# Expert weights in pieces of 256 rows by 1024 columns, two chunks at once, and a ScalarE loop that begins at the gathered copies

## What is computed

```
def moe_swiglu(h, router, w1, w3, w2):
    logits = (h @ router).astype(jnp.float32)
    top_vals, top_idx = lax.top_k(logits, TOP_K)
    top_w = jax.nn.softmax(top_vals, axis=-1)
    combine = jnp.sum(jax.nn.one_hot(top_idx, N_EXPERTS) * top_w[..., None], axis=-2)
    for e in range(N_EXPERTS):
        y = y + combine[..., e:e+1] * ((silu(h @ w1[e]) * (h @ w3[e])) @ w2[e])
```

## Time and profile before

| what | value |
|---|---|
| median of 3 runs | 1594.7 us (1590.41 to 1596.37) |
| profiled execution | 1590.57 us, span 1588.8 us |
| TensorE matmul (PE) busy | 1520.4 us, 96% |
| VectorE (DVE) busy | 1181.2 us, 74% |
| ScalarE (ACT) busy | 906.5 us, 57% |
| read from HBM | 424.31 MB |
| expert weights (ring<-in_moe_w) | 336 transfers of 1 MB |
| expert loop on TensorE | from 594 us to the last scatter at 1580 us |

### The profile page before, as it was taken

One profiled execution on the slowest core, in us unless ns is written; L12 is line 12 of the kernel. 1 busy time (PEld: TensorE's weight loads), 2 busy tenths in 40 slices (PEclk: granted clock), 3 DMA queues, 4 the chain that ended last, 5 costly groups with the idle time before them and its releaser, 6 DMA issues.

```text
span 1588.8 us, 19808 instructions
## 1 busy us (share of the span) xinstructions
PE 1520.4 (96%) x7386; PEld 1211.3 (76%) x7386; DVE 1181.2 (74%) x1148; ACT 906.5 (57%) x830; POOL 29.9 (2%) x44
## 2 busy tenths in 40 slices
PE   7987999998997889999999999999999999999998
PEld 5654599997654478888887888888888888888886
DVE  4974354453884348889888889888889888889895
ACT  1034243441013347777777777778777778777774
POOL 1010000000011000000000000000000000000000
PEclk9987999999996989999999999999999999999999
DMA  7540365635170039999999999998999999999992
GB/s 250 198 150 0 117 202 186 191 101 186 36 257 1 0 135 341 377 369 364 360 364 321 372 380 351 363 375 315 369 375 356 368 362 328 360 378 367 364 362 87
DMA packets 203556, 426.58 MB, mean 268 GB/s; under 512 B 7378, under 2 KB 48594, under 8 KB 203476
## 3 DMA queue, kind: packets, MB, share of 16 engines
q1 hardware_dynamic: 202160, 424.90, 74.5%
q10 hardware_dynamic: 1316, 0.49, 0.1%
HBM read 424.31 MB, written 1.05 MB: 268 GB/s over the span
## 4 chain that ended last, share of the span: by engine, by line
PE 89%; DVE 5%; issue 2%; ACT 2%; DMA 1%; POOL 0%; ACTq 0%; POOLq 0%; DVEq 0%; SPq 0%
PE bank L1520 13%; PE bank L1522 13%; PE bank L1521 13%; PE bank L1164 8%; PE bank L1544 6%; PE bank L1542 6%; PE bank L1543 6%; PE bank L1421 3%; PE bank L1422 3%; PE bank L1423 3%; PE bank L1351 2%; PE bank L1530 2%; PE bank L1439 1%; PE bank L1438 1%; PE bank L1437 1%
## 5 line engine op out<-in xcount | busy, mean ns | idle before, releaser
L761 DVE TENSOR_TENSOR w_split<-ring,w_split 128x2048 fp32r<-128x2048 f32 x369 | 843.1, 2290 | 201.6 <-ACT w_split L504 200.8
L504 ACT CAST w_split<-ring 128x2048 fp32r<-128x2048 f32 x369 | 705.4, 1914 | 287.7 <-PE bank L1522 160.0
L1520 PE MATMUL bank<-w_split,xe_hi 128*128 128x512 f32 x896 | 355.6, 397 | 6.9 <-DVE w_split L761 6.9
L1522 PE MATMUL bank<-w_split,xe_lo 128*128 128x512 f32 x896 | 350.3, 391 | 0.0
L1521 PE MATMUL bank<-w_split,xe_hi 128*128 128x512 f32 x896 | 349.7, 390 | 0.0
L1520 PEld LDWEIGHTS bank<-w_split,xe_hi 128*128 128x128 f32 x896 | 168.7, 188 | 42.7 <-DVE w_split L761 9.2
L1522 PEld LDWEIGHTS bank<-w_split,xe_lo 128*128 128x128 f32 x896 | 168.6, 188 | 36.4
L1521 PEld LDWEIGHTS bank<-w_split,xe_hi 128*128 128x128 f32 x896 | 168.8, 188 | 33.3
L1542 PE MATMUL bank<-w_split,actT_hi 128*128 128x512 f32 x448 | 175.2, 391 | 0.0
L1544 PE MATMUL bank<-w_split,actT_lo 128*128 128x512 f32 x448 | 174.5, 389 | 0.0
L1543 PE MATMUL bank<-w_split,actT_hi 128*128 128x512 f32 x448 | 174.4, 389 | 0.0
(11 more groups left out here) (229 smaller groups left out, 1362.1 us busy)
## 6 DMA issues: line engine op xcount, KB each, us to landing
ring<-in_moe_w SPq DMA_DIRECT2D x336, 1024.0 KB, 6.5
ring<-in_dense_w SPq DMA_DIRECT2D x33, 1024.0 KB, 5.3
ring<-in_w_in SPq DMA_DIRECT2D x8, 1024.0 KB, 10.1
ring<-in_w_in SPq DMA_DIRECT2D x4, 2048.0 KB, 13.9
ring<-in_w_out SPq DMA_DIRECT2D x4, 2048.0 KB, 13.7
ring<-in_cmp_k_w SPq DMA_DIRECT2D x2, 2048.0 KB, 16.1
ring<-in_cmp_v_w SPq DMA_DIRECT2D x2, 2048.0 KB, 8.3
ring<-in_w_in SPq DMA_DIRECT2D x2, 1120.0 KB, 14.9
```

The costliest lines, as they stand in the source:

```text
L504: nc.scalar.copy(split_part(0, t), raw(t)).then_inc(w_hi_ready, 1)
L761: V.tensor_tensor(split_part(1, t), raw(t), split_part(0, t).bitcast(F32), ALU.subtract).then_inc(w_lo_ready, 1)
L1520: T.matmul(dst, xe_hi[:, kk, own], hi[:, k, :], start=(kk == 0), stop=False)
L1522: last = T.matmul(dst, xe_lo[:, kk, own], hi[:, k, :], start=False, stop=(kk == KD - 1))
```

## The change

An expert's first and third matrix are read in pieces of 256 rows by 1024 columns, which serve two chunks at once (the seventh chunk stays alone, with pieces of 512 by 512). The chunks form four groups (0, 1), (2, 3), (4, 5), (6); e1 and e3 of a group fill two banks each. The order of pieces, the matmuls' order, the places of the gates, of the gate products, of the adds, of the scatter and of the selection follow from the groups. The scatter uses bank 4 in place of 3. On ScalarE the five gathered copies 3 to 7 move from the end of a loop turn to the head of the next, behind the small activation that names the silu table, and after the loop they stand once more.

Numbered from 0, the 42 pieces of an expert are then: e1(0, 1) 0 to 3, e3(0, 1) 4 to 7; e1(2, 3) 8 to 11, e2(0) 12, 13, e3(2, 3) 14 to 17, e2(1) 18, 19; e1(4, 5) 20 to 23, e2(2) 24, 25, e3(4, 5) 26 to 29, e2(3) 30, 31; e1(6) 32, 33, e2(4) 34, 35, e3(6) 36, 37, e2(5) 38, 39, e2(6) 40, 41.

```diff
-    expert_stream = [("e1", 0, 0), ("e1", 0, 1), ("e3", 0, 0), ("e3", 0, 1)]
-    for c in range(1, FCH):
-        expert_stream += [("e1", c, 0), ("e1", c, 1), ("e3", c, 0), ("e3", c, 1), ("e2", c - 1, 0), ("e2", c - 1, 1)]
-    expert_stream += [("e2", FCH - 1, 0), ("e2", FCH - 1, 1)]
+    groups = [tuple(range(c, min(c + 2, FCH))) for c in range(0, FCH, 2)]
+    expert_stream = []
+    for g, own in enumerate(groups):
+        before_it = groups[g - 1] if g else ()
+        for kind, n in (("e1", 0), ("e3", 1)):
+            expert_stream += [(kind, own[0], q) for q in range(2 * len(own))]
+            expert_stream += [("e2", c, half) for c in before_it[n:n + 1] for half in range(2)]
+    expert_stream += [("e2", FCH - 1, half) for half in range(2)]
...
-        BACK = (3, 5, 6, 7)
+        BACK = (4, 5, 6, 7)
...
-                        src = (w1 if kind == "e1" else w3)[:, 4 * half:4 * half + 4, c * BANK:(c + 1) * BANK]
-                        dst = raw(t).rearrange("p (k n) -> p k n", k=4)
+                        wide = len(groups[c // 2])
+                        k = 4 // wide
+                        src = (w1 if kind == "e1" else w3)[:, k * half:k * half + k, c * BANK:(c + wide) * BANK]
+                        dst = raw(t).rearrange("p (k n) -> p k n", k=k)
```

ScalarE:

```diff
-            for q in range(2 * QB):
+            for q in range(3):
                 gathered(0, q)
...
             with sc.Fori(0, pairs) as pair:
+                nc.scalar.activation(cstat[:, 1:2], ones[:, 0:1], ACT.Silu)
+                for q in range(3, 2 * QB):
+                    gathered(pair, q)
...
+                    for g, chunks in enumerate(groups):
+                        c, last = chunks[0], 2 * len(chunks) - 1
+                        if g >= 1:
+                            highs(done, past("e1", c, last // 2))
+                            actT_high(c - 2)
+                            done = past("e1", c, last // 2)
+                        highs(done, past("e1", c, last))
+                        done = past("e1", c, last)
+                        used("e1", c, last)
+                        for n in chunks:
+                            gate(n)
+                        if g >= 1:
+                            highs(done, past("e2", c - 2, 1))
+                            done = past("e2", c - 2, 1)
+                            actT_high(c - 1)
+                        if g == 2:
                             sc.wait_ge(selT_psum, nth(j, 1, 1))
...
-                    if h == PAIR - 1:
-                        for q in range(3, 2 * QB):
-                            gathered(pair + 1, q)
+            for q in range(3, 2 * QB):
+                gathered(pairs, q)
```

VectorE:

```diff
+                    def lows(first, end):
+                        for t in range(first, end):
+                            low_part(BASE + t, j)
+                            if t == 2:
+                                scaled_low(j)
+
+                    def past(kind, c, half):
+
+                        return min(xplace[kind, c, half] + SPLIT + 1, XS)
+
                     done = 0
-                    for c in range(FCH):
...
+                    for g, chunks in enumerate(groups):
+                        c, last = chunks[0], 2 * len(chunks) - 1
+                        if g >= 1:
+                            lows(done, past("e1", c, last // 2))
+                            actT_low(c - 2)
+                            done = past("e1", c, last // 2)
+                            lows(done, past("e2", c - 2, 1))
+                            done = past("e2", c - 2, 1)
                             actT_low(c - 1)
...
+                        ready = min(xplace["e3", c, last] + SPLIT, XS - 1)
+                        lows(done, ready)
+                        done = ready
+                        for n in chunks:
+                            dv.wait_ge(sg_ready, nth(j, FCH, n + 1))
+                            if n == c:
+                                used("e3", c, last)
+                            V.tensor_tensor(act[:, n % 2, :], sg[:, n % 2, :], bank[2 + n % 2][:],
+                                            ALU.mult).then_inc(act_ready, 1)
+                        if g == 0:
+                            add_back(j)
+                        if g == 1 and h == PAIR - 1:
+                            dv.wait_ge(selT_psum, nth(j, 1, 1))
+                            select(pair + 1)
```

TensorE (`select_rows` holds what stood at L1573 to L1579):

```diff
+                    up("e1", 0, range(4))
                     scatter(j)
-                    for c in range(1, FCH):
-                        up("e1", c)
+                    up("e3", 0, range(4))
+                    for c in range(2, FCH, 2):
+                        pieces = 2 * len(groups[c // 2])
+                        pe.wait_ge(sg_ready, nth(j, FCH, c))
+                        up("e1", c, range(pieces // 2))
+                        if c == 2:
+                            pe.wait_ge(added, nth(j, 4, 2))
+                        transposes(c - 2)
+                        up("e1", c, range(pieces // 2, pieces))
+                        if c == 2:
+                            pe.wait_ge(added, nth(j, 4, 5))
+                        down(c - 2, 0)
+                        down(c - 2, 1)
                         transposes(c - 1)
+                        up("e3", c, range(pieces))
...
                         down(c - 1, 1)
                         if c == 2:
+                            select_rows()
```

More of the change, by code:

```diff
@@ L669, in actT_high, with gate @@
                         nc.scalar.copy(actT_hi[:, c % 2, :], bank[4][:]).then_inc(actT_hi_ready, 1)
-                    done = 0
-                    for c in range(FCH):
[L673 to L683, removed]
+                    def gate(c):
                         if c >= 2:
@@ L686, in _, with highs @@
                         nc.scalar.activation(sg[:, c % 2, :], bank[c % 2][:], ACT.Silu).then_inc(sg_ready, 1)
-                        if c == 3:
+                    def highs(first, end):
+                        for t in range(first, end):
+                            high_part(BASE + t, j)
+                            if t == 2:
+                                scaled_high(j)
+                    def past(kind, c, half):
+                        return min(xplace[kind, c, half] + SPLIT + 1, XS)
+                    done = 0
+                    for g, chunks in enumerate(groups):
[14 more added lines that the diff above has]
+                        if g == 2:
                             sc.wait_ge(selT_psum, nth(j, 1, 1))
@@ L690, in _ @@
                             nc.scalar.copy(slot_weight[:], bank[7][:, S:S + 1]).then_inc(selT_ready, 1)
-                    while done < xplace["e2", FCH - 1, 0]:
-                        high_part(BASE + done, j)
-                        done += 1
+                    highs(done, xplace["e2", FCH - 1, 0])
                     if h == PAIR - 1:
@@ L1107, in actT_low @@
                                         ALU.subtract).then_inc(actT_ready, 1)
-                    done = 0
[L1110 to L1117, removed]
-                            actT_low(c - 1)
[L1119 to L1126, removed]
+                    def lows(first, end):
+                        for t in range(first, end):
+                            low_part(BASE + t, j)
+                            if t == 2:
+                                scaled_low(j)
@@ new lines, in past @@
+                    def past(kind, c, half):
+                        return min(xplace[kind, c, half] + SPLIT + 1, XS)
+                    done = 0
+                    for g, chunks in enumerate(groups):
[6 more added lines that the diff above has]
+                            done = past("e2", c - 2, 1)
+                            actT_low(c - 1)
+                        ready = min(xplace["e3", c, last] + SPLIT, XS - 1)
[8 more added lines that the diff above has]
+                        if g == 0:
@@ L1127, in _ @@
                             add_back(j)
-                        if c == 3 and h == PAIR - 1:
+                        if g == 1 and h == PAIR - 1:
                             dv.wait_ge(selT_psum, nth(j, 1, 1))
                             select(pair + 1)
-                    while done <= xplace["e2", FCH - 1, 0]:
-                        low_part(BASE + done, j)
-                        done += 1
+                    lows(done, xplace["e2", FCH - 1, 0] + 1)
                     actT_low(FCH - 1)
@@ L1510, in split_piece, with up @@
                         return split_views(t, k)
[L1512 to L1522, removed]
+                    def up(kind, c, pieces):
+                        wide = len(groups[c // 2])
+                        for q in pieces:
+                            hi, lo = split_piece(kind, c, q, 4 // wide)
+                            for k in range(4 // wide):
+                                kk = 4 // wide * q + k
+                                for n in range(wide):
```

(27 more changed lines are left out.)

## The result

The changed kernel took 1645.1 us (median of 4, 1644.1 to 1646.3) against 1595.4 for the kernel before on the same chip: a ratio of 1.0318, 95% interval 1.0295 to 1.0341 (a ratio here is estimated from all the runs; the quotient of the two medians is 1.0311). The forecast was 1644.

What follows compares the result with a forecast made beforehand. TensorE was taken to bound the kernel; waits of 14.1, 13.2 and 16.1 us plus 6.4 for the clock gave 49.8 on 1590.57, or 1640.4, and 4.1 more for the median: forecast 1644, own range 1630 to 1656, wider range 1614 to 1666.

Steps and rivals of the forecast that it cites:

- Wait A: Before piece 10, every expert: low 10 queues behind two gate products and four adds on VectorE; 1.77 us, eight times.
- Wait C: Before piece 34, every expert: VectorE subtracts the needed activations only after low 35; 2.01 us, eight times, 16.1 us.
- Wait B: Before piece 20, each pair's second expert: low 20 stands behind a selection awaiting TensorE; 3.31 us, four times, 13.2 us.
- The clock: TensorE's 3.2 us idle before piece 20 brings a half-clock stretch costing 1.6 us, four times, 6.4 us.
- Transfers, groups, bank 4 at 0: Longer transfer runs, places that hold despite the wider groups, and the scatter's new bank: each forecast to cost 0.
- ScalarE's head at 0: Between pairs: one table load per pair falls away but gains 0, because TensorE's own loop branch ends the gap.
- clock at all waits: Rival: half clock also follows the waits at pieces 10 and 34, up to 25.6 us more, 1670 us; chance 0.15.
- A and C covered: Rival: one more piece in hand hides the waits at pieces 10 and 34, giving 1614 us; chance 0.12.
- The transfers pace the loop: Rival: weight transfers limit the expert loop and hide TensorE's stalls, so time stays at 1594.7 us; chance 0.05.
- ScalarE at the heads: Rival: ScalarE's lateness at loop heads holds TensorE, VectorE's order costs nothing; 7.4 us gained, 1587.3 us; chance 0.03.

Runs made afterwards that it cites:

- e1: Not a run in the kept text: the matmuls with an expert's first matrix, as in e1(0, 1), pieces 0 to 3; no time of its own.
- e3: Not a run in the kept text: the matmuls with an expert's third matrix, as in e3(0, 1), pieces 4 to 7; no time of its own.
- fillers at all three: Changed kernel with unused identity transposes on TensorE before piece 10, before piece 34 and before piece 20 of the second expert; 1638.6 us, ratio 1.0299.
- all three edits: Changed kernel with selection one group later, scatter behind e3 and chunk 4's activations a piece earlier; 1594.8 us against 1592.3 for the kernel before, ratio 1.0014.
- the head alone: Kernel before with only ScalarE's new loop head (table-naming activation first, gathered copies 3 to 7 behind it); 1592.9 us against 1593.2, ratio 0.9994.
- again: The changed kernel unaltered, measured once more beside the kernel before on the same chip; 1648.1 us, ratio 1.0344.
- selection later: Changed kernel with VectorE writing the next pair's selection one group later, behind the subtraction of chunk 2's transposed activations; 1627.1 us, ratio 1.0227.
- last group: Changed kernel with chunk 4's transposed activations cast and subtracted one weight piece earlier, before the high and low part of piece 35; 1624.3 us, ratio 1.0202.
- filler at B: Changed kernel with 26 unused identity transposes in TensorE's wait at piece 20, second expert of each pair; 1640.5 us, ratio 1.0304.
- scatter back: Changed kernel with the scatter moved from between e1 and e3 of the first group to behind e3; 1636.2 us, ratio 1.0292.
- selection early: Kernel before with only VectorE's selection for the next pair moved from chunk 3 to chunk 2; 1615.8 us, ratio 1.0133.

## Why the prediction was right

- *TensorE bounds, so each wait counts in full.* Shown: taking away one wait at a time shortens the loop by 21.2, 21.4 and 12.6 us, and taking away all three brings back the 983.6 us. That the three numbers add up to just the 55.2 of the change is partly chance: each also holds what the clock did in that profile, and two of them the 1.6 us at the loop's start. The waits alone, 13.8, 16.5 and 14.2, are 44.5, against the 44.6 of the run with fillers at all three.
- *Wait A:* forecast 1.77 a time, 14.1 in all; measured 1.77, 14.2. *Wait C:* forecast 2.01 and 16.1; measured 2.06 and 16.5. *Wait B:* forecast 3.31 and 13.2; measured 3.44 and 13.8. B's 0.13 a time is a step that I had taken as 0.05: from the end of the selection's matmuls (778.26 + 0.50) to VectorE's first select (778.93) it is 0.17. The three together: forecast 43.4, measured 44.6. (The first term, 8 x 1.77, is 14.2 and stands as 14.1 in the sum; it changes nothing.)
- *The clock:* the mis-sized term. Forecast 6.4 (four stretches of 3.2 us), measured 10.5. In the changed kernel half clock came behind all four waits B, as forecast, but for 3.4 us once and 6.8 us three times; and behind one of the eight waits C, where I had taken none. The price of a stretch held roughly: 10.5 us for 27.3 us at half clock, of which some 4 fell into the waits B themselves. What was wrong was their length and number.
- *Transfers, groups, bank 4 at 0:* right, by the run with all three edits.
- *ScalarE's head at 0:* right, and by the named cause. (What follows the table load at once, at 836.84 us in the kernel before, is a weight's cast, and not the copies' cast that the forecast names.)
- *The sum:* 1640.4 was forecast for the profiled execution, which took 1645.2; the clock gives 4.1 more than forecast and the waits 1.2, and outside the loop the changed kernel's profile was some 0.6 us shorter. The forecast of the median came nearer than that, 1644 for 1645.1, and this part is luck: I had added 4.1 because the profiled execution of the kernel before lay that far under its median, and the changed kernel's lay at its own.
- *The rivals:* clock at all waits: no as stated, for it fell at A never and at C once in eight. It was not an empty rival, though: in the five profiles that keep wait C without a filler, half clock followed it 10 times in 40. A and C covered: no, TensorE waits at both. The transfers pace the loop: no, they slowed from 361 to 342 GB/s with it, no cast waited for a landing, SyncE waited for ring places most of the time, and a stretch with 417 GB/s shows that 361 is not their limit. The rule cited from the Trainium skill (DMA: Bandwidth & Descriptors, section Where 436 GB/s comes from) would have hidden the waits. Its 358 GB/s is there half of what a memory stack gives to two cores; one core ran here, and the measured 417 lies above it. ScalarE at the heads: no, by the run with the head alone.

No version here beats the kernel before: its expert loop has no idle time within a turn, and what is left between turns are three gaps of some 1.5 us, which end with TensorE's own branch.

## What to carry to other kernels

Where one engine is busy without a gap and its feeders run in an order written by hand, draw up each feeder's queue between two deadlines of the bound engine, and add the durations: three reorderings, each of which looked free by busy share (VectorE at 88% of a turn), cost 44.6 us, and the sums said so to within 3%. Look above all for a wait in the feeder that the bound engine can end only just before it needs the feeder again. Grouping two steps into one doubles what is queued ahead of the next deadline, so the cover that stood there (here a scatter) must stay where the burst is.

## What was not expected of the hardware

The same idle time of TensorE is not always followed by the same clock. The table counts the gaps of each kind in the profiles that have it without a filler; a gap is from matmul to matmul.

| gap | half clock followed | profiles |
|---|---|---|
| wait A, 1.79 us | 0 of 40 | changed kernel, again, selection later, last group, filler at B |
| wait C, 2.18 us | 10 of 40 (1, 0, 2, 5, 2 of 8) | changed kernel, again, selection later, scatter back, filler at B |
| wait B, 3.55 us | 20 of 20, for 3.4 us (10 times) or 6.8 us (10 times) | changed kernel, again, last group, scatter back, selection early |
| ahead of the first piece, 3.66 us | 9 of 11, for 3.4 us | all |

So the length of a gap does not settle it: the longest of these four was passed twice at full clock. What decides between two gaps of one length no run here shows. Filling a wait with transposes that nobody reads kept the clock at 2.4 GHz and gave back 10.5 us of 55.
